# Moving the gate row of the first block out of the opening stage and into two projections

## The reference, cut to what matters

```python
c_act = jax.nn.silu(c)
for i in range(DEPTH):                       # DEPTH = 2
    mod = c_act @ w_ada[i] + b_ada[i]        # (1024) @ (1024, 6144)
    sh1, sc1, g1, sh2, sc2, g2 = [m[:, None, :] for m in jnp.split(mod, 6, axis=-1)]
    h = rmsnorm(x, mix_norm[i]) * (1.0 + sc1) + sh1
    y = fox_mixer(...)                       # i = 0:  h @ w_in, attention, o @ w_out
    x = x + g1 * y
    h = rmsnorm(x, ffn_norm[i]) * (1.0 + sc2) + sh2
    x = x + g2 * hier_moe(...)
```

## Time and profile before

| | |
|---|---|
| median of 3 runs | 3376.74 us (3369.96 to 3378.46) |
| the profiled execution | 3375.21 us |
| its span in the profile | 3373.3 us |
| TensorE busy | 2960.6 us (88% of the span) |
| VectorE busy | 2424.2 us (72%) |
| ScalarE busy | 1316.2 us (39%) |
| opening stage | 0 to 64.06 us |
| fox_in | 64.06 to about 231 us |
| fox_out | 383.3 to about 444 us |

### The profile page before, as it was taken

How to read it: one execution, slowest core, us unless ns; L and a number is a source line. 1 busy time by engine, 2 the same in 40 slices (tenths; PEclk the granted TensorE clock), 3 DMA queues, 4 the chain that set the end, 5 groups by cost and what they waited for, 6 DMA issues and landing times. The chain is left out here.

```text
span 3373.3 us, 45111 instructions
## 1 busy us (share of the span) xinstructions
PE 2960.6 (88%) x15395; PEld 2406.3 (71%) x15395; DVE 2424.2 (72%) x3995; ACT 1316.2 (39%) x2282; POOL 832.5 (25%) x606
## 2 busy tenths in 40 slices
PE   7889969997799599989589677888879999999996
PEld 4886756665677466647356666888868888888885
DVE  3867765556587656579868568689867777777778
ACT  2325434443564254312422232555523333333332
POOL 0001100130021002300022023667623443343431
PEclk9999979998899799999789878999989999999998
DMA  6861468984205699812000122265488888888885
GB/s 265 321 247 31 142 239 346 350 318 167 66 0 188 253 349 346 306 58 81 10 29 14 57 82 74 95 204 179 128 294 326 312 319 333 323 314 328 324 326 202
DMA packets 221123, 703.79 MB, mean 209 GB/s; under 512 B 21771, under 2 KB 100620, under 8 KB 202020
## 3 DMA queue, kind: packets, MB, share of 16 engines
q1 hardware_dynamic: 174022, 480.47, 39.3%
q0 software_dynamic: 46944, 221.27, 18.0%
HBM read 645.54 MB, written 56.13 MB: 208 GB/s over the span
## 5 line engine op out<-in xcount | busy, mean ns | idle before, releaser
L500 PE MATMUL peer_chunks_low<-peer_chunks_down_hi,peer_chunks_bent_hi 128*128 128x512 f32 x768 | 299.5, 390 | 3.0 <-DVE peer_chunks_bent_lo L3151 2.9
L502 PE MATMUL peer_chunks_low<-peer_chunks_down_hi,peer_chunks_bent_lo 128*128 128x512 f32 x768 | 300.4, 391 | 0.0
L501 PE MATMUL peer_chunks_low<-peer_chunks_down_lo,peer_chunks_bent_hi 128*128 128x512 f32 x768 | 300.2, 391 | 0.0
L3023 POOL DMA_INDIRECT peer_chunks_got_up<-in_peer_u_rows,peer_rows_at x128 | 207.1, 1618 | 314.8 <-DVE peer_chunks_got_up L3155 289.8
L500 PE MATMUL peer_chunks_risen<-peer_h_hi,peer_chunks_up_hi 128*128 128x384 f32 x640 | 216.3, 338 | 4.1 <-DVE peer_chunks_up_lo L3132 3.9
L502 PE MATMUL peer_chunks_risen<-peer_h_hi,peer_chunks_up_lo 128*128 128x384 f32 x640 | 215.9, 337 | 0.0
L501 PE MATMUL peer_chunks_risen<-peer_h_lo,peer_chunks_up_hi 128*128 128x384 f32 x640 | 215.4, 337 | 0.0
L3029 POOL DMA_INDIRECT peer_chunks_got_down<-in_peer_v,peer_rows_at x128 | 131.1, 1024 | 242.5 <-DVE mod L3167 236.1
L3132 DVE TENSOR_TENSOR peer_chunks_up_lo<-hT,peer_chunks_up_hi 128x1024 fp32r<-128x1024 f32 x80 | 98.0, 1224 | 111.9 <-ACT peer_chunks_up_hi L3084 111.6
L500 PEld LDWEIGHTS peer_chunks_low<-peer_chunks_down_hi,peer_chunks_bent_hi 128*128 128x128 f32 x768 | 144.3, 188 | 33.3 <-issue 5.0
L3167 DVE SCALAR_TENSOR_TENSOR mod<-peer_chunks_got_down,peer_chunks_shares,mod 128x1024 f32<-128x1024 f32 x128 | 164.1, 1282 | 4.2 <-DVE peer_chunks_shares L3160 1.2
(11 more groups left out here) (683 smaller groups left out, 8510.9 us busy)
## 6 DMA issues: line engine op xcount, KB each, us to landing
moe_raw<-in_moe_gate_up SPq DMA_DIRECT2D x32, 2048.0 KB, 9.6
hT<-in_peer_v SPq DMA_DIRECT2D x128, 512.0 KB, 5.4
hT<-in_peer_u SPq DMA_DIRECT2D x112, 512.0 KB, 7.0
fox_o<-in_side_w SPq DMA_DIRECT2D x80, 512.0 KB, 5.8
peer_w<-peer_ahead_stage SPq DMA_DIRECT2D x24, 1024.0 KB, 7.3
peer_chunks_weights<-peer_w SPq DMA_DIRECT2D x128, 192.0 KB, 5.4
mla_o<-in_side_w SPq DMA_DIRECT2D x40, 512.0 KB, 5.2
moe_raw_dn<-in_moe_down SPq DMA_DIRECT2D x16, 1024.0 KB, 8.8
```

The costliest lines, as they stand in the source:

```text
L500: nc.tensor.matmul(out, l_hi, r_hi, start=start, stop=False)
L501: nc.tensor.matmul(out, l_hi, r_lo, start=False, stop=False)
L502: return nc.tensor.matmul(out, l_lo, r_hi, start=False, stop=stop)
L3023: pool.indirect_dma_start(got_up[:, c % GOT], None, a["peer_u_rows"], bass.IndirectOffsetOnAxis(ap=rows_at[:, c:c + 1], axis=0)).then_inc( ...
```

## The change

The gate row leaves the opening. Its pieces 4 and 5 are no longer loaded and summed there; TensorE's order is then the four pieces of scale and shift, and the transposes. Instead the gate row becomes row 0 of the side sums, which are now 16 rows; in fox_in there are nine of them, 72 steps, and `share` becomes ceil(72 / 11) = 7, so seven steps beside pieces 0 to 9 and two beside piece 10. Its bias still lies in `g.mod[:, 2]` from the opening. In fox_out a new object `GateRow` loads the partial sums of row 0 back (512 KB), TensorE sums them over the partitions in two matmuls of 128x512 after its piece 0 and waits until VectorE has added both to `g.mod[:, 2]`; only then the six matmuls of `LateRows` follow. VectorE does these two additions after its side sums of piece 0 and before it gates piece 0. In all other stages only the numbers of the rows move by one; the work is the same.

```diff
-    ORDER, SLOTS, SHIFT, SCALE = (2, 3, 0, 1, 4, 5), 3, 0, 1
+    ORDER, SLOTS, SHIFT, SCALE = (2, 3, 0, 1), 3, 0, 1
...
-                for n in range(len(ORDER) - 1):
+                for n in range(len(ORDER)):
                     sum_(n)
...
-                sum_(len(ORDER) - 1)
...
-                add_bias(4)
-                add_bias(5)
...
+class GateRow(Beside):
+
+    def __init__(self, nc, s, g, late):
+        self.nc, self.g, self.late = nc, g, late
+        self.sums = s.sb("gate_sums", [P, D])
+        self.gate_in, self.gate_summed, self.gate_kept = s.sem("gate_in"), s.sem("gate_summed"), s.sem("gate_kept")
+
+    def sync(self, sp, n):
+        if n == -1:
+            sp.dma_start(self.sums[:], self.g.side_sums[0]).then_inc(self.gate_in, 16)
+
+    def tensor(self, pe, n):
+        if n == 0:
+            pe.wait_ge(self.late.filled, 1)
+            pe.wait_ge(self.gate_in, 16)
+            for half in range(D // BANK):
+                self.nc.tensor.matmul(self.late.banks[half], self.late.ones[:], self.sums[:, half * BANK:(half + 1) * BANK],
+                                      start=True, stop=True).then_inc(self.gate_summed, 1)
+            pe.wait_ge(self.gate_kept, D // BANK)
+
+    def vector(self, dve, n):
+        if n == 0:
+            for half in range(D // BANK):
+                columns = self.g.mod[:, 2, half * BANK:(half + 1) * BANK]
+                dve.wait_ge(self.gate_summed, half + 1)
+                self.nc.vector.tensor_tensor(columns, self.late.banks[half], columns, ALU.add).then_inc(self.gate_kept, 1)
+            dve.wait_ge(self.gate_kept, D // BANK)
...
-                        SideSums(nc, s, g, a["side_w"], o, 0, 8, chunks, acc=g.next[:, :2]),
+                        SideSums(nc, s, g, a["side_w"], o, 0, 9, chunks, acc=g.next[:, :2]),
...
-                     beside=lambda s, acc, l_split, kept: [SideSums(nc, s, g, a["side_w"], o, 8, 2, D // HALF), Moments(nc, s, g, "rms", D // HALF),
-                                                          LateRows(nc, s, g, a["side_b"], 0, g.next, [acc[:, 1, 2], acc[:, 1, 3]], gain=a["ffn_gain"][0])])
+        def beside_out(s, acc, l_split, kept):
+            late = LateRows(nc, s, g, a["side_b"], 1, g.next, [acc[:, 1, 2], acc[:, 1, 3]], gain=a["ffn_gain"][0])
+            return [SideSums(nc, s, g, a["side_w"], o, 9, 2, D // HALF), Moments(nc, s, g, "rms", D // HALF),
+                    GateRow(nc, s, g, late), late]
+
+        project_rows(nc, g, "fox_out", None, KD, out_of, rows=o, gate=g.mod[:, 2], x=g.x, beside=beside_out)
```

More of the change, by code:

```diff
@@ L24 @@
 HALF = 256
-HALF_ROWS, LATE_ROWS = 3, 15
+HALF_ROWS, LATE_ROWS = 3, 16
 EPS = 1e-6
@@ L298, in add @@
         row, k, u = n // KD, n % KD, n % self.RING
-        c = self.g.c_act[:, 0 if self.first + row < 9 else 1, k:k + 1]
+        c = self.g.c_act[:, 0 if self.first + row < 10 else 1, k:k + 1]
         acc = self.acc[:, row % 2]
@@ L3244, in build_program @@
         g.mod, g.next = g.next, g.mod
-        moe(nc, g, a, 0, late=3)
+        moe(nc, g, a, 0, late=4)
         g.mod, g.next = g.next, g.mod
@@ L3249, in build_program @@
         g.mod, g.next = g.next, g.mod
-        moe(nc, g, a, 1, late=9)
+        moe(nc, g, a, 1, late=10)
         g.mod, g.next = g.next, g.mod
@@ L3297, in fox @@
                       v, o, FOX_DK, a["fox_gains"], cum_q=cum_q, cum=sums, spare=1, early_loads=out_of.load)
-        project_rows(nc, g, "fox_out", None, KD, out_of, rows=o, gate=g.mod[:, 2], x=g.x,
-                     beside=lambda s, acc, l_split, kept: [SideSums(nc, s, g, a["side_w"], o, 8, 2, D // HALF), Moments(nc, s, g, "rms", D // HALF),
-                                                          LateRows(nc, s, g, a["side_b"], 0, g.next, [acc[:, 1, 2], acc[:, 1, 3]], gain=a["ffn_gain"][0])])
+        def beside_out(s, acc, l_split, kept):
[3 more added lines that the diff above has]
+        project_rows(nc, g, "fox_out", None, KD, out_of, rows=o, gate=g.mod[:, 2], x=g.x, beside=beside_out)
 def mla(nc, g, a):
@@ L3310, in mla @@
         project_rows(nc, g, "mla_in", g.hT, KD, into,
-                     beside=lambda s, acc, l_split, kept: [SideSums(nc, s, g, a["side_w"], o, 10, 2, 2)])
+                     beside=lambda s, acc, l_split, kept: [SideSums(nc, s, g, a["side_w"], o, 11, 2, 2)])
         with ExitStack() as own:
@@ L3351, in mla @@
         project_rows(nc, g, "mla_out", None, KD, out_of, rows=o, gate=g.mod[:, 2], x=g.x,
-                     beside=lambda s, acc, l_split, kept: [SideSums(nc, s, g, a["side_w"], o, 12, 3, D // HALF),
+                     beside=lambda s, acc, l_split, kept: [SideSums(nc, s, g, a["side_w"], o, 13, 3, D // HALF),
                                                           Moments(nc, s, g, "rms", D // HALF, square=idle[:, :HALF]),
-                                                          LateRows(nc, s, g, a["side_b"], 6, g.next, [acc[:, 1, 2], acc[:, 1, 3]], gain=a["ffn_gain"][1],
+                                                          LateRows(nc, s, g, a["side_b"], 7, g.next, [acc[:, 1, 2], acc[:, 1, 3]], gain=a["ffn_gain"][1],
                                                                    gain_at=idle[:, HALF:HALF + D])])
@@ L3429, in hybrid @@
         project_rows(nc, g, "hybrid_out", None, KD, out_of, rows=y, gate=g.mod[:, 2], x=g.x, alpha=ALPHA,
-                     beside=lambda s, acc, l_split, kept: [LateRows(nc, s, g, a["side_b"], 12, g.next, [acc[:, 1, 2], acc[:, 1, 3]], sums=sums),
+                     beside=lambda s, acc, l_split, kept: [LateRows(nc, s, g, a["side_b"], 13, g.next, [acc[:, 1, 2], acc[:, 1, 3]], sums=sums),
                                                               Moments(nc, s, g, "ln", D // HALF)])
@@ L3489, in laid_out @@
         "positions": in_columns(x["positions"][0]),
-        "w_ada0": row_chunks(x["w_ada"][0][:, :HALF_ROWS * D], BANK), "b_ada": x["b_ada"][0:1, :HALF_ROWS * D],
-        "side_w": np.concatenate([side_rows(w) for w in (x["w_ada"][0][:, HALF_ROWS * D:], x["w_ada"][1], x["cond_w_2"])]),
-        "side_b": np.concatenate([x["b_ada"][0][HALF_ROWS * D:], x["b_ada"][1], x["cond_b_2"]]).reshape(LATE_ROWS, D),
+        "w_ada0": row_chunks(x["w_ada"][0][:, :2 * D], BANK), "b_ada": x["b_ada"][0:1, :HALF_ROWS * D],
+        "side_w": np.concatenate([side_rows(w) for w in (x["w_ada"][0][:, 2 * D:], x["w_ada"][1], x["cond_w_2"])]),
+        "side_b": np.concatenate([x["b_ada"][0][2 * D:], x["b_ada"][1], x["cond_b_2"]]).reshape(LATE_ROWS, D),
         "mix_gain": everywhere(x["mix_norm"]), "ffn_gain": everywhere(x["ffn_norm"]),
```

## The result

The kernel after takes 3406.67 us (median of 4 runs, 3395.03 to 3416.45) against 3373.36 us before: +33.3 us, ratio 1.0096 with a 95% interval of 1.0057 to 1.0135. Measured again beside other kernels it took 3401.07 us (median of 7 runs) against 3376.43 (of 24), ratio 1.0052 (1.0027 to 1.0078). So it is slower, as forecast, but by 25 to 33 us in place of 13.7. The profiled execution is the shortest of the first four, 3395.03 us with a span of 3393.2 us.

The account below looks back on a forecast made before the run. It took fox_in as bound by a chain from transfers through side sums and cuts to pieces. Opening -11.0, fox_in +15.6, fox_out +7.3 and +1.8 gave +13.7 us: 3390.4 us against the median of 3376.74, range 3379 to 3397.

Parts of the forecast that it names:

- Part 1: Opening: without the gate row's matmuls, loads and additions, fox_in begins at 53.0 us, saving 11.0 us; bounds -11.0 and -10.0.
- the prediction's own exception: Opening: if TensorE transposes at its lower clock, the tail gets 1 us longer, so the gain is 10.0 us.
- Part 2: fox_in: ten more steps and one more store ahead of the last piece's cut add 15.6 us by transfers.
- the high bound of 17.5: fox_in: added 5.77 MB at the average 351 GB/s give 16.4 us, plus one microsecond for a lower-clock start.
- I take 15.6, since the transfers are the fuller of the two: fox_in: transfers need 13.95 us a period against VectorE's 12.6, so their sum, 15.6 us, was chosen over VectorE's 13.3.
- Part 3: fox_out: TensorE waits for VectorE's gate additions ahead of the late matmuls, 7.3 us, plus 1.8 for clock; bounds 6.5 and 11.
- the 1.8: fox_out: after 6.3 us idle, TensorE runs about 3.6 us at 1.2 GHz, costing half of that, 1.8 us.
- Rival 1: fox_in: added steps ride in VectorE's waits, the stage grows under 2 us, total about 3377 us; chance 0.13.
- rival 2: fox_out: the gate's wait is short or taken back, costing 0 to 2 us, total 3382 us; chance 0.12.
- rival 3: Only the opening counts: fox_in and fox_out hardly grow, sum -9 us, total 3368 us; chance 0.03.
- Rival 4: fox_in: TensorE's clock goes down there too after idle time before pieces, sum +17 us, total 3394 us; chance 0.14.
- the two signs by which the prediction called itself wrong: fox_in's period stays near 13.2 us, or fox_out's late matmuls start within 3 us of the gate's.

Follow-up runs that it names:

- opening_only: The kernel after with the gate row left out altogether, so eight side-sum rows in fox_in and no gate object in fox_out: 3374.39 us, ratio 0.9982 to before.
- six_steps: The kernel after with six side-sum steps beside each of fox_in's twelve pieces, so 60 lie ahead of the last cut: 3392.48 us, ratio 1.0041 to before.
- gate_behind: The kernel after with TensorE doing fox_out's six late matmuls first and the gate row's two behind them: 3402.59 us, ratio 1.0067 to before.

## Why the prediction was wrong

**Part 1, the opening, -11.0 us.** The mechanism is right, and the first profile shows 11.1 us. But eleven profiles with the new opening begin fox_in between 52.9 and 55.9 us, 54.4 on average, three with the old one at 63.5: the gain is 9.1 us on average, outside the bounds of 10 to 11. Two things differ. In six of the eleven the times of the transposes add up to 11.1 us in place of 8.9; opening_only, one of them, had a granted clock of 0.84 from 45 to 56 us, the first profile 1.00 from 45 to 53. That is the prediction's own exception. And the shift row was complete between 45.7 and 47.5 us, with the old opening between 44.2 and 45.9. Whether the early loads of fox_in's weights had a part in that wasn't tried.

**Part 2, fox_in, +15.6 us: the term that failed.** It measured 24.1 us between the first two profiles, and 173.3 - 152.9 = 20.4 us between the means of four and two, above the high bound of 17.5. The step that fails is "I take 15.6, since the transfers are the fuller of the two", with the prices under it: 1.28 us for a load and 2.8 us for a store. Taking ten loads away gave back 3.6 us, taking eight stores 10.9, and a fifth slot, which takes away nothing, 14.1. A DMA share of 1.00 in one period and the waits for loads had been read as a limit of the engines' rate. What the runs show in its place is the ring: four slots, each taken for the load's whole way, and a SyncE that issues a load only when a slot comes free. The numbers were in the trace before: the way is 6.0 us in the median there too, and 59 of the 60 loads behind the first four were issued within 0.21 us of the end of the step that freed their slot. By the estimate above ten steps cost 18 us; six_steps measured 18.4, a store included. (The Trainium skill, HBM Reference, Specifications, has about 425 GB/s for a core that streams alone. The ring kept this stage at 333 from cut to cut, and with the fifth slot it came to 373, stores included.) The high bound was made from the average rate and so left the ring out. The 2.8 us for a store was read from 3.6 us in which no load was issued either, between 136.99 and 140.98 us, while VectorE was at its reduction and its cut.

The growth is not spread evenly. In the last seven of the nine periods it is 103.00 - 90.47 = 12.5 us, 1.8 a period, and a period is 14.7 us, as forecast. That agreement is luck: it starts from 12.9 us, not from the 13.2 that all nine average, and rises by 1.8, not by 1.5. The first two periods grew by 9.0 us and what lies ahead of them by 2.6; most of what exceeds the 15.6 is there. TensorE's waits for the cut, 25.2 us, also came near the forecast 26 by luck: its matmuls, at a granted clock of 0.91 in place of 1.00, were busy for 114.3 us in place of 107.7 and so filled 6.6 us of longer periods.

**Part 3, fox_out, +9.1 us.** Right in place, order and cause, a little short in size and within its bounds: 10.5 us. VectorE came to the addition 1.65 us later than reckoned, 1.12 us of it because its side sums waited for a load, so that TensorE stood for 8.02 us and not 6.3; and the lower clock took 7.68 - 5.70 = 2.0 us of the late matmuls, near the 1.8.

**The rivals.** Rival 1 (the steps ride in VectorE's waits) and rival 2 (a short wait in fox_out) are out, and with them rival 3; rival 2 is what gate_behind makes. Rival 4 came in part: the granted clock in fox_in fell from 0.99 to 0.92, and ahead of the last copy of the first profile it shows: 243.75 - 228.15 - 2.28 = 13.3 us against 11.9. Neither of the two signs by which the prediction called itself wrong came: the period did not stay near 13.2 us, and the late matmuls did not start within 3 us of the gate's.

**The sum.** The stages give -9.1 + 20.4 + 10.5 = +21.8 us by averages, 8.1 above the forecast: 1.9 from the opening, 4.8 from fox_in, 1.4 from fox_out. The second measurement, +24.6 us, fits this. The first profile gives -11.1 + 24.1 + 1.4 (the last piece) + 3.0 + 10.5 = +27.9 us up to the next norm. The 3.0 is the attention, from fox_in's last copy to fox_out's first cast 156.6 in place of 153.6 us; profiles of other kernels, in which it is the same too, have either length, so it is no part of the change. Behind that norm nothing was changed, and yet the fourteen profiles took between 2919 and 2948 us there; the first profile of the kernel after took 2921 and the one of the kernel before 2929, so that the profiled execution as a whole is only 19.8 us longer. Of the +33.3 of the first measurement some 5 to 12 us are therefore left, and that spread is wide enough for them in a median of four. The two longest of the four, 3416.45 and 3412.01 us, also have the lowest granted clocks, 0.929 and 0.931 against 0.936 and 0.933, as the execution with the long scan had 0.931. That long scans caused them wasn't seen, since they were not profiled.

**What stays open.** Between the kernels with five slots the ninth row costs 159.2 - 141.7 = 17.5 us, against 20.4 with four, and profiles differ by 3 us. So the fifth slot shows what holds the level of the stage in both kernels; that the ring also makes the difference between 15.6 and 20.4 us isn't shown. Why the first two of the nine periods grew most, to 17.3 and 20.1 us from 13.7 and 14.6, wasn't tried; with five slots they took 14.7 and 15.6, with small stores 14.9 and 16.2. And with five slots every load was still issued at once when its slot came free, so the ring may hold the stage still; six slots weren't tried.

## What to carry to other kernels

Where an engine waits for its loads and the transfer engines look nearly full, compare three numbers before pricing one more step: its bytes by the rate, its compute time, and the time from issue to landing plus compute divided by the slots of the ring. Take the largest as a first estimate, and look at who releases the next load: if it is the end of a step, one more slot is the cheap test. And put a wait for a busy engine behind the independent work in the same queue, not ahead of it: here that order alone was worth 8 us in its stage, though the time of the whole did not show it.

## What had not been expected of the hardware

A load of 16 columns per partition in place of 1024 saved about 0.4 us of the chain per load (3.6 us for ten, give or take 3), although the rate of the engines made it worth 1.28 us. A busy share of the transfer engines of 0.94 went with 234 GB/s in one stretch of 2 us and one of 1.02 with 416 in another. And TensorE's granted clock in a stage that no edit touched moved that stage from 166.5 to 182.6 us (0.96 against 0.87), in two profiles of one kernel in which it begins within 0.7 us of the same time; three profiles of fourteen show the long form, two one of 172 us.
